# A decoder layer in one kernel: first head's turn reordered, decay mask on POOL, halves of the inverse interleaved, last stage's gate chunks prepared elsewhere

## What is computed

```python
h = rmsnorm(x, attn_norm);  proj = h @ w_in       # 1024 x 9232
qa, ka, va, qb, kb, vb, zb, bb, ab, gl = split(proj)
# 8 heads of differential attention, blocks of 128 queries, causal, T5 bias
w  = softmax(q0 k0' + bias) - lam * softmax(q1 k1' + bias);  oa = rmsnorm(w @ va)
# 8 heads of gated DeltaNet in chunks of C = 64 tokens
A  = I + strict_lower(k_beta k' * decay)          # 64 x 64 per head and chunk
u, w = triangular_solve(A, [v_beta, k_beta * exp(g)])
attn_intra = tril(q k' * decay);  state = ...;  ob = rmsnorm(o) * silu(zb)
x = x + (sigmoid(gl0) * (oa @ w_br_a) + sigmoid(gl1) * (ob @ w_br_b)) @ w_out
x = x + (silu(conv(h @ w_up)[gate]) * conv(...)[value]) @ w_down
x = x + sigmoid(rmsnorm(x) @ w_ple_gate) * (p @ w_ple_proj)
```

## Time and profile before

| what | value |
|---|---|
| median of three runs | 1157.43 us (1157.13 to 1157.69) |
| the profiled execution | 1157.37 us |
| its span, first to last instruction | 1155.6 us |
| mean granted clock of PE | 0.999 |
| busy: PE, DVE, ACT, POOL | 1121.9, 659.6, 550.9, 640.3 us |
| PE's share of the span | 97% |

### The profile page before, as it was taken

The page is one execution under the profiler, slowest core; times in us unless marked ns, Lnnn a source line. Parts: engine busy times, 40 slices in busy tenths (PEclk is TensorE's granted clock), DMA queues, the critical chain, the costliest instruction groups (busy, mean ns, idle before and its releaser), DMA issues.

```text
span 1155.6 us, 16770 instructions
## 1 busy us (share of the span) xinstructions
PE 1121.9 (97%) x5498; PEld 898.1 (78%) x5498; DVE 659.6 (57%) x1043; ACT 550.9 (48%) x888; POOL 640.3 (55%) x769
## 2 busy tenths in 40 slices
PE   6999989999999999999999999999999999999998
PEld 4786667777777777667878888888888888888876
DVE  4567977767666776862213324576776515731644
ACT  4584657566565656551322124544444314433542
POOL 6476255646554564645456554576576744573452
PEclk9999999999999999999999999999999999999999
DMA  8255031331404123223223523233333432332223
GB/s 244 69 138 133 17 102 39 82 88 32 103 17 119 36 66 101 73 56 88 77 76 107 182 73 91 85 104 113 100 91 91 120 99 73 109 96 78 77 80 89
DMA packets 196636, 104.36 MB, mean 90 GB/s; under 512 B 3943, under 2 KB 195418, under 8 KB 196570
## 3 DMA queue, kind: packets, MB, share of 16 engines
q1 hardware_dynamic: 196188, 103.39, 32.1%
q10 hardware_dynamic: 381, 0.15, 0.0%
HBM read 101.40 MB, written 2.13 MB: 90 GB/s over the span
## 4 chain that ended last, share of the span: by engine, by line
PE 41%; POOL 25%; issue 23%; DVE 8%; ACT 3%; DMA 1%; POOLq 0%; SPq 0%; DVEq 0%; ACTq 0%
PE bank L567 30%; POOL w_lo L497 25%; PE bank L703 2%; PE bank L717 1%; DVE prod L1818 1%; DVE xs L1820 1%; PE bank L710 1%; PE bank L662 1%; DMA x_tok<-in_x 1%; PE bank L927 1%; DVE pr L1730 1%; DVE oa_lo L1986 0%; PE bank L914 0%; DVE pr L1729 0%; PE bank L924 0%
## 5 line engine op out<-in xcount | busy, mean ns | idle before, releaser
L497 POOL TENSOR_TENSOR w_lo<-w_raw,w_hi 128x256 fp32r<-128x256 f32 x692 | 556.5, 838 | 255.6 <-ACT w_hi L1080 249.8
L567 PE MATMUL bank<-hn_hi,w_hi 128*128 128x512 f32 x1000 | 407.7, 408 | 2.5 <-POOL w_lo L497 1.6
L567 PE MATMUL bank<-hn_hi,w_lo 128*128 128x512 f32 x1000 | 391.0, 391 | 0.0
L567 PE MATMUL bank<-hn_lo,w_hi 128*128 128x512 f32 x1000 | 390.4, 390 | 0.0
L567 PEld LDWEIGHTS bank<-hn_hi,w_hi 128*128 128x128 f32 x1000 | 189.0, 189 | 45.4 <-issue 10.6
L567 PEld LDWEIGHTS bank<-hn_hi,w_lo 128*128 128x128 f32 x1000 | 188.0, 188 | 40.3
L567 PEld LDWEIGHTS bank<-hn_lo,w_hi 128*128 128x128 f32 x1000 | 188.8, 189 | 34.2 <-issue 1.2
L512 POOL CAST w_hi<-w_raw 128x1024 fp32r<-128x1024 f32 x70 | 78.8, 1126 | 216.6 <-PE bank L567 125.6
L1080 ACT ACTIVATE w_hi<-w_raw 128x1024 fp32r<-128x1024 f32 x111 | 117.9, 1062 | 77.7 <-PE bank L567 69.8
L2111 DVE SCALAR_TENSOR_TENSOR u<-vr,pt,u 128x511 f32<-128x511 f32 x88 | 90.5, 1029 | 8.0 <-DVE u L2111 0.2
L567 PE MATMUL bank<-fa_hi,w_hi 128*128 128x512 f32 x176 | 68.5, 389 | 0.0
(11 more groups left out here) (313 smaller groups left out, 1645.0 us busy)
## 6 DMA issues: line engine op xcount, KB each, us to landing
w_raw<-in_w_in SPq DMA_DIRECT2D x73, 512.0 KB, 6.8
w_raw<-in_w_up SPq DMA_DIRECT2D x44, 512.0 KB, 3.7
w_raw<-in_w_down SPq DMA_DIRECT2D x16, 512.0 KB, 3.9
crow<-cum_rows_out SPq DMA_DIRECT2D x16, 256.0 KB, 5.8
w_raw<-in_w_br_a SPq DMA_DIRECT2D x8, 512.0 KB, 3.9
w_raw<-in_w_br_b SPq DMA_DIRECT2D x8, 512.0 KB, 3.9
w_raw<-in_w_out SPq DMA_DIRECT2D x8, 512.0 KB, 4.0
w_raw<-in_w_ple_gate SPq DMA_DIRECT2D x8, 512.0 KB, 4.1
```

Source lines behind the costliest of these rows:

```text
L497: ins = pool.tensor_tensor(wlo[c.slot][:, ks, :], raw[c.slot][:, ks, :], whi[c.slot][:, ks, :].bitcast(F32), ALU.subtract)
L567: mm = pe.matmul(acc, w[c.slot][:, i, :], xx[:, x0 + i, :], start=(i == 0 and n == 0), stop=last)
```

## The change

Lead turn: `prep(0, 1)` goes ahead of the scaling of `li`, PE does two steps ahead of `scores(0, 0)` instead of one, and `substitute` is cut in smaller portions; columns 20 to 30 and `turn_back` move into turn 0. Turn 0: `pair_low` moves behind `scores(1, 1)`, the softmax of blocks 0 and 1 ahead of the inverse's copies on ACT, and `combine(1, 1)` ahead of the products of the DeltaNet on DVE. The decay mask goes from DVE to POOL, and POOL does four weight chunks ahead of its copies of the turned blocks instead of one. The halves of the inverse: low half g+1 and high half g are issued alternately as one group, which makes five slots (`halves(-1)` a lone low half, `halves(0)` to `halves(2)` shared, `halves(3)` a lone high half) instead of eight. Last stage: `gather(stage, 6)` moves behind the last product, one step and the order of `first_two` change, and `high(ple.at(3))` moves from the first `ple_turn` ahead of the root.

```diff
-STEPS_FIRST = ((2, 4, 1, 9, 1, 8, 1, 8), ((1, 1), (1, 1, 1), (1, 1, 1), (1, 1, 1)))
+STEPS_FIRST = ((2, 4, 1, 10, 1, 8, 1, 8), ((1, 1), (1, 1, 1), (1, 1, 1), (1, 1, 1)))
@@ POOL
+            pool.wait_ge(sem("dec"), 1)
+            pool.tensor_tensor(dec[:, :, :], dec[:, :, :], cum.unsqueeze(1).to_broadcast([P, NT, P]),
+                               ALU.mult).then_inc(sem("dec_cut"), 1)
             for h in range(H - 2):
                 for n in range(len(TURN)):
                     both(stream.heads[h].at(n))
-                    if h == 0 and n == 0:
+                    if h == 0 and n == 3:
                         pool.wait_ge(sem("turned_back"), 2)
@@ PE
+            def halves(g):
+                pe.wait_ge(sem("placed"), 2 if g < 0 else 6)
+                pe.wait_ge(sem("pairs"), 1 if g < 1 else 2)
+                if g >= 0:
+                    pe.wait_ge(sem("inverse_ui"), g + 3)
...
+                for n in range(8):
+                    if g < H // 2 - 1:
+                        low = low_half(8 * g + 8 + n)
+                    if g >= 0:
+                        high = high_half(8 * g + n)
@@ PE, turn(h), around scores(a, 1) and behind
-                f.step(before[1] - 2 if h == 0 else before[1])
+                f.step(before[1])
-                if h == 0:
-                    for g in range(2):
-                        pair_low(g)
-                        f.step(1)
+                if h == 0:
+                    f.step(7)
+                    pair_low(0)
+                    f.step(1)
+                    pair_low(1)
+                    f.step(before[3] - 8)
+                    turn_w(a, 1)
+                    f.step(before[4])
...
+                if 0 < h < H // 2:
+                    halves(h)
...
+                if h == 0:
+                    halves(-1)
...
+                if h == 0:
+                    f.step(3)
+                    halves(0)
+                    f.step(before[7] - 3)
@@ PE, first_two
-                run(gemm(c, hn_hi, hn_lo, ready=("n_split", stage * KD)))
+                one = Fill(gemm(c, hn_hi, hn_lo, ready=("n_split", stage * KD)))
                 f = Fill(gemm(then, x_hi, x_lo, k))
-                f.step(2)
+                one.step(KD - 1)
+                f.step(1)
+                one.rest()
+                f.step(1)
@@ ACT, turn(h)
-                if h == 0:
-                    pair_copy(0)
-                    pair_copy(1)
...
+                        first_tap(a, 0, at("qb"))
+                        place_rows()
+                    keep_w(a, 1)
+                        pair_copy(0)
+                        pair_copy(1)
...
+                    if 0 < h < H // 2:
+                        half_take(h)
                     softmax(a, 2)
+                    if h == 0:
+                        pair_sign(0)
+                        pair_sign(1)
+                        keep_w(a, 2)
+                        place_columns()
+                        half_copy(0)
                     first_tap(a, 2, at("vb"))
@@ ACT, norm_r and the last stage
+                if stage == 1:
+                    high(stream.ple.at(3))
...
+            ple_turn(0, 4, 1)
+            with act.Fori(1, KD // 2 - 1) as n:
@@ DVE, lead_turn(at) and turn(h)
-                substitute(13, 18)
+                substitute(9, 14)
                 prep(1, 0)
-                substitute(18, 24)
-                steps(finish_silu(0, 2))
+                substitute(14, 20)
                 attention_scale(0)
-                substitute(24, 28)
-                first_mask()
                 prep(1, 1)
-                substitute(28, 31)
-                turn_back()
...
+                if h == 0:
+                    maxima(a, 0)
+                    substitute(20, 21)
+                    combine(a, 0)
+                    substitute(21, 31)
+                    turn_back()
+                    maxima(a, 1)
+                    turn_again()
+                    combine(a, 1)
+                    scaled_keys()
+                    scaled_values()
```

182 lines of the change are left out of this document (90 added, 92 removed).

## The result

The changed kernel took 1162.22 us (median of seven runs, 1159.55 to 1163.41), the kernel before 1157.82 in the same comparison: a ratio of 1.0038, 95% interval 1.0029 to 1.0047. It is 4.4 us slower. The forecast was 1161.6 and slower.

The account below looks back on a forecast made before the run. PE was taken as the bound, busy 1121.9 of 1155.6 us. New waits of 16.6 against 7.9 (+8.7), halves -3.2 and last stage -1.25 summed to +4.2: 1161.6 us, likeliest range 1160 to 1163.7, whole range 1153.0 to 1164.5.

Parts of the forecast that it names:

- Lead turn: Lead turn: PE's waits of 2.46 and 1.51 us go, except some 0.8 at turn_w(0, 1): -3.2 us.
- Price of the contention: DVE's substitution beside POOL's weight work: a middle column's operation takes 0.86 us instead of a pitch of 0.45.
- scores(1, 0): Turn 0: PE waits 3.3 us before scores(1, 0) instead of 0.84, as POOL holds up DVE; bounds 0 and 3.7.
- pair_low: Turn 0, behind scores(1, 1): pair_low(0) waits 3.3 us for the transpose behind columns 21 to 30; range 2.7 to 4.1.
- turn_w(1, 1): Turn 0: PE waits 2.0 us for DVE's maxima, second transpose and combine; range 1.3 to 3.4.
- scores(1, 2): Turn 0: PE waits 3.3 us for keep_w(1, 1), behind first_tap and place_rows in ACT's queue; independent of POOL.
- Halves: Inverse's halves: five slots instead of eight, paired halves running side by side, 3 x 1.07: -3.2 us.
- the clock is no matter: Whole kernel: the granted clock, 0.999 throughout in the profile before, was left out of the forecast.
- Clean overlap: Rival, turn 0: POOL's work doesn't hold DVE up, so the change is faster, 1154.4 us; chance 0.29.
- Half of it: Rival, turn 0: half the POOL-DVE contention, 3.6 us, gives 1158.0 us; chance 0.15.
- Halves in series: Rival, shared slots: the two halves don't overlap, +3.2 us, 1164.8 us; chance 0.06.
- the last stage does nothing: Rival, last stage: the 1.57 wait moves on or ACT's table load replaces it, +1.25 us, inside the range; no separate chance.

Follow-up runs that it names:

- POOL's number alone: Kernel before with one number changed: POOL does four weight chunks instead of one ahead of its copies, mask still on DVE; 1161.45 us, ratio 1.0039.
- mask late: Changed kernel with the decay mask behind the fourth weight chunk in POOL's queue instead of ahead of the first; 1159.64 us, ratio 1.0018.
- `keep_w` first: Changed kernel with ACT's keep_w(1, 1) ahead of the first tap and place_rows; 1161.01 us, ratio 1.0030 to the kernel before.
- PE kept busy: Changed kernel with 12 unread transposes on PE ahead of scores(1, 0) and 12 ahead of pair_low(0); 1161.57 us, ratio 1.0032.
- halves in series: Changed kernel with the eight low and eight high products of a shared slot one group behind the other, not alternately; 1162.89 us, ratio 1.0045.
- PE kept busy with three blocks: Changed kernel with unread transposes on PE: 12 ahead of scores(1, 0), 12 ahead of pair_low(0), 16 ahead of scores(1, 2); 1163.75 us, ratio 1.0042.

## Why the prediction was right, and where it was not

**Right in sign and sum**: +4.2 forecast, +4.4 measured. By its steps:

- *Lead turn*, -3.2: it was -4.4. The 0.8 that I kept at `turn_w(0, 1)` wasn't there, PE ran through both places, which makes 4.0; where the other 0.4 came from I haven't found.
- *Price of the contention*, 0.86 per operation: 0.86 measured. This rests on two rows of 87 columns that told it for 250 columns, and the run with POOL's number alone shows that it causes the loss. POOL's end at about 157 was 154.8 (and 1.3 of that is the trace's earlier start).
- *scores(1, 0)* 3.3 and *pair_low* 3.3: 2.62 and 2.48, within or just under my bounds (0 to 3.7; 2.7 to 4.1). DVE was done with the columns earlier: POOL was already out of work at 154.8, so only six operations of turn 0's met it. The second number is right by luck: PE's own way from `scores(1, 0)` to `pair_low(0)`, which I put at 13.8, took 13.7, but with the dip behind 146.15 in it. In two kernels whose clock stayed up there (mask late, `keep_w` first) it takes 12.1 to 12.2, and they wait over 4 us. The two `pair_low` groups that move away cost not 1.5 but some 2.8 (8.4 us from `scores(1, 0)` to `turn_w(1, 0)` with them, 5.6 without, both at the full clock).
- *turn_w(1, 1)* 2.0: **wrong**. There was no wait; PE came 1.1 us after DVE, at half the clock. At the full clock the way from `pair_low(0)` takes 4.8 us (163.60 to 169.68 less the wait of 1.27, in the kernel with PE kept busy), not 3.6; so with the clock up there would have been a wait for DVE of about 1.2 (an estimate).
- *scores(1, 2)* 3.3: 1.75, since PE came late there for the same reason (3.27 in the kernel with PE kept busy, whose clock was up on the way there). ACT's queue was what it waited for, as said.
- *turn_w(1, 3)* 2.2: 2.36. *Head of turn 1* 1.7: 0.75, and 0.52 one block later.
- *Halves* -3.2: -3.7; besides the 1.07 of the slot some 0.2 go with each, which I take for the gaps at its two borders. *Last stage* -1.25: -1.1.

The step that failed is the sentence that the clock is no matter. It was read off one execution of the kernel before, whose longest wait in these turns is 2.46. The waits that I had added up grew by only 2.6 us (10.5 against 7.9) where I had +8.7. In the profiled execution the low clock (4.5 us) and the later turns' 1.1 filled most of the gap, with the head start of 1.3 against them, and it came out at +2.2 us beside the profiled kernel before. That the median is +4.4, next to my 4.2, is luck: errors that cancel, and slower runs of which I had no idea. The ACT order of the later turns (`ob_r` behind `keep_w`) I had not costed at all.

The profiled execution is 2.7 us faster than the median. The runs' mean granted clocks are 0.994 for it and 0.990 to 0.993 for the six others. 0.002 less over 1160 us is 2 x 0.002 x 1160 = 4.6 us more at half the clock, worth up to 2.3 us. That is the right size, but the run at 0.993 was the slowest, so this is a reading and not a proof. For it speaks that four near relatives of the changed kernel (mask late, `keep_w` first, halves in series, PE kept busy with three blocks) show one more dip behind the wait at `turn_w(1, 3)`, near 200 us, where the changed kernel's trace has none.

**The rivals.** Clean overlap fell with the pitch. Half of it fell too. Halves in series fell with the row of 188.46. That the last stage does nothing fell with the wait of 0.42.

## What to carry to other kernels

Before work is put on an idle GpSimd, look at what VectorE does in that idle time: with two inputs in SBUF it runs at the pitch of GpSimd's operations, and one number in a queue can cost 4.7 us. An operation with a late input at the head of a queue is a gate for all behind it, and there can be a second gate behind the first: here the mask in POOL's queue and a row load in SP's waited for the same operation on ACT. And if a change makes new waits on TensorE, price the low clock behind them as well: 9.7 us at half speed cost 4.3 us where PE was the bound, and nothing that could be measured where PE would have waited for another engine anyway.

## What the runs showed of the hardware that I had not expected

- The granted clock fell to 0.50 in turn 0 of every variant with one of the change's new waits there, for 3 to 10 us at a time (3.4 behind `scores(1, 0)` and 6.8 behind `pair_low(0)` in the changed kernel, 10.2 around the end of the wait of 7.10), but not behind each wait (the kernel with `keep_w` first kept it up behind 2.62 us), and once behind a wait of 1.38 with small transposes ahead of it.
- POOL is slowed by the contention as well: 3.42 for four pieces against 2.81 to 2.88.
- Two 64x64 products in disjoint quarters, issued alternately, take the time of one: 32 passes in 1.08 us, against 1.83 with one group behind the other.
- With the mask out of its way POOL still waited 9.96 us for a chunk's DMA, because the issue stood in SP's queue behind one that waited 19.2 us for ACT. So a chunk can't be moved forward at will.
